# One kernel of four residual blocks on Trainium2: attention and retention of two mixers woven between weight units, gate sums and experts' one-hots moved

## The chip, the cores and the metric

The kernel runs on one core of one Trainium2 chip. Its five engines take instructions from queues of their own: TensorE (PE) multiplies, VectorE (DVE) and ScalarE (ACT) do elementwise work, GpSimd (POOL) and SyncE (SP) here only start DMAs. An engine runs its queue in the order in which the program was written; semaphores tie the queues together. The metric is the device time in microseconds of one execution; lower is better.

## The reference, cut to what matters

The input x is 256 rows by 1024. Everything is float32.

```
for l in 0, 1:                                  # first block
    mod = silu(c) @ ada_w[l] + ada_b[l]         # 6 vectors of 1024: sh1 sc1 g1 sh2 sc2 g2
    x += g1 * hybrid_mixer(rms_norm(x)*(1+sc1)+sh1)
    h  = rms_norm(x)*(1+sc2)+sh2
    x += g2 * (swiglu(h, 2816 wide) if l == 0 else moe_ffn(h))   # 8 experts, top 2
x = rms_norm(x)
for l in 0, 1:                                  # second block
    x += 0.5 * swiglu(rms_norm(x))              # ffn1, 2816 wide
    x += even_mixer(x) if l == 0 else odd_mixer(x)
    x += 0.5 * swiglu(rms_norm(x))              # ffn2
hybrid_mixer: h @ w_in (1024 x 3584) -> q k v of 8 heads of 64, q k v gate of 4 heads of 128
    causal softmax attention on the first, normed; rotary and decayed retention on the second,
    normed per head, times silu(gate); both side by side (1024) @ w_out (1024 x 1024)
```

## The kernel before

**Weights.** All weights pass through the core once, in *units* of 512 KB: 256 rows of a weight by 512 columns (or 128 rows by 1024). SP loads them into a ring of 12 raw buffers. A float32 product is made of three passes with rounded parts: ACT writes `hi`, the rounded weight (line 296), DVE writes `lo`, raw minus hi (line 298), and PE does hi by hi, hi by lo and lo by hi (`passes`, line 317, 128x512 each). There are SPL = 6 buffers of hi and of lo. So hi of unit u waits until PE has freed unit u-6; the semaphore `unit_free` counts that. How far ahead of PE the splits stand in the queues of ACT and DVE is written in the program: `split_to(n)` issues the splits up to unit n, `look_ahead(n)` the next n.

**Order of stages** (times of the profiled execution): conditioning to 60.8 us; hybrid mixer 0 to 240.9; dense ffn 0 to 476; hybrid mixer 1 483 to 655.9; routing to 705; the experts to 1530; then ffn1.0, the even mixer, ffn2.0, ffn1.1, the odd mixer and ffn2.1, which ends at 2622.

**Hybrid mixer.** `project` makes seven slabs of 512 columns with four units each; tile t = 0 of a slab (rows 0 to 127) is done for all four units, then t = 1. Heads are turned (transposed on PE) after the third and the sixth slab. Then `attention` runs 8 heads with no weights between them: scores on PE (line 1108), mask and maximum on DVE, two exps on ACT, a turn on PE (line 1154, 4 transposes), a copy on ACT, values on PE (line 1172). Two banks take turns for scores and two for turns. Retention follows, then the norms, and w_out (8 units) with `project_out`.

**Ada sums.** The vectors mod are products with one row, so DVE does them: it multiplies a 128x512 piece of `ada_w` by a column of c and adds it up (lines 270, 273, 844); PE then sums over partitions (lines 852, 957, 962). 32 units of `ada_w` lie in the raw ring between the weights of mixer 0 ("acc" units); the 12 slabs of layer 1 come by POOL's own DMAs, 11 of them beside the 11 steps of ffn 0 and the last beside mixer 1.

**Dense ffn.** A *step* takes six units: four for gate and up, 256 columns of the hidden each, and two for down of the step before. PE does gate and up of tile 0, the turn of the hidden (line 425), gate and up of tile 1, then down (`pe_down`), whose first product waits for `hidT_lo` (DVE, line 435), and that for `hidT_hi` (ACT, line 433). Each weight unit is freed in the part for tile 1, in down by its last product. After the last step `pe_down_last` does tile 0 and then tile 1, and the additions to x (DVE) and the next stage's first turns follow.

**Experts.** 88 steps of eight experts, 11 each, in the same manner for 128 rows. Two experts form a pair. At the second expert of a pair `one_hots(p+1)` (DVE, 4 instructions) and `gather` (PE, line 1746) prepare the next pair; at the first, `turn_one_hots` (PE, lines 1773 and 1776) prepares the way back.

## Time and profile before

| | us |
|---|---|
| median of 3 runs | 2629.36 (2629.26 to 2630.66) |
| the profiled execution, device time | 2626.93 |
| its span in the trace | 2625.7 |
| PE busy | 2383.0 (91%) |
| DVE busy | 1783.2 (68%) |
| ACT busy | 1377.8 (52%) |
| mean granted clock of TensorE | 0.924 of full |

Busy time is the union of an engine's instructions. A row that ends in brackets gives the idle time of the engine before it and the instruction that ended it. The three passes of a full-speed product start 0.2275 us apart, at half clock 0.427 us apart, though each is drawn 0.39 or 0.63 us long, since they overlap. A unit for both tiles is 12 passes, 2.73 us.

### The profile page before, as it was taken

The page shows a single profiled execution, that of the slowest core. Times are in us where ns is not written, and L with a number is a line of the kernel's source. Part 1 is how long each engine was busy: PE and PEld are TensorE (multiplying, and loading weights), DVE is VectorE, ACT ScalarE, POOL GpSimd, SP SyncE. Part 2 cuts the span into 40 slices and gives each one's busy share as a digit, 9 for nine tenths or more (in the row PEclk, how much of TensorE's full clock was granted, in tenths as well). Part 3 has the DMA queues.
Part 4 walks back from the last instruction along what each step waited for, and adds up shares of the span by engine and source line. Part 5 has one row for each costly group of instructions (what it writes and reads, how often), then busy time and mean ns, then how long its engine had stood idle before and what let it go on. Part 6 is the DMA issues. An engine that isn't in the chain of part 4 may idle for free.

```text
span 2625.7 us, 35352 instructions
## 1 busy us (share of the span) xinstructions
PE 2383.0 (91%) x10593; PEld 1953.9 (74%) x10593; DVE 1783.2 (68%) x2330; ACT 1377.8 (52%) x1955; POOL 47.9 (2%) x77
## 2 busy tenths in 40 slices
PE   6987899798499999999999979998899999869998
PEld 5766687677387877877878858876788788747887
DVE  5786777564398988988889965558555555575554
ACT  4333443243277767767767754444544544533543
POOL 1000111100000000000000000000000000000000
PEclk8968999897599999999999989998899999958999
DMA  8773788351199999999999955543356555311651
GB/s 293 238 240 100 263 299 301 107 176 40 49 346 315 368 308 328 356 311 363 318 308 368 368 188 191 188 154 127 122 184 190 164 188 179 131 56 44 196 182 59
DMA packets 410160, 571.51 MB, mean 218 GB/s; under 512 B 28103, under 2 KB 324465, under 8 KB 409938
## 3 DMA queue, kind: packets, MB, share of 16 engines
q1 hardware_dynamic: 399024, 538.94, 61.6%
q0 software_dynamic: 8112, 28.18, 3.6%
q10 hardware_dynamic: 2930, 3.22, 0.4%
q8 instruction: 50, 0.82, 0.1%
q14 instruction: 44, 0.36, 0.0%
HBM read 569.18 MB, written 1.05 MB: 217 GB/s over the span
## 4 chain that ended last, share of the span: by engine, by line
PE 80%; DVE 12%; ACT 4%; issue 2%; DMA 1%; SPq 0%; DVEq 0%; ACTq 0%; POOLq 0%
PE bank L317 70%; DVE lo L298 3%; PE bank L1108 1%; DVE small L90 1%; PE bank L1172 1%; DVE xn L90 1%; PE bank L425 1%; DVE proj L90 1%; PE bank L1746 1%; DVE aT_lo L90 1%; ACT xn L90 1%; PE bank L1154 1%; PE bank L1694 1%; DMA ada_slot<-ada_w 1%; DVE hT_full L90 1%
## 5 line engine op out<-in xcount | busy, mean ns | idle before, releaser
L298 DVE TENSOR_TENSOR lo<-raw,hi 128x1024 fp32r<-128x1024 f32 x997 | 1172.5, 1221 | 172.7 <-ACT hi L296 158.8
L296 ACT ACTIVATE hi<-raw 128x1024 fp32r<-128x1024 f32 x997 | 999.7, 1054 | 129.8 <-PE bank L317 121.7
L317 PE MATMUL bank<-hi,aT_hi 128*128 128x512 f32 (+2 forms) x2064 | 828.2, 401 | 20.0 <-DVE lo L298 9.2
L317 PE MATMUL bank<-hi,aT_lo 128*128 128x512 f32 (+2 forms) x2064 | 807.9, 391 | 0.0
L317 PE MATMUL bank<-lo,aT_hi 128*128 128x512 f32 (+2 forms) x2064 | 806.8, 391 | 0.0
L317 PEld LDWEIGHTS bank<-hi,aT_hi 128*128 128x128 f32 x2064 | 391.6, 190 | 104.6 <-issue 12.1
L317 PEld LDWEIGHTS bank<-hi,aT_lo 128*128 128x128 f32 x2064 | 390.5, 189 | 82.5
L317 PEld LDWEIGHTS bank<-lo,aT_hi 128*128 128x128 f32 x2064 | 391.9, 190 | 79.0 <-issue 3.1
L317 PE MATMUL bank<-hi,hidT_hi 128*128 128x512 f32 x792 | 315.6, 398 | 6.6 <-DVE hidT_lo L435 5.6
L317 PE MATMUL bank<-lo,hidT_hi 128*128 128x512 f32 x792 | 313.7, 396 | 0.0
L317 PE MATMUL bank<-hi,hidT_lo 128*128 128x512 f32 x792 | 312.9, 395 | 0.0
L317 PEld LDWEIGHTS bank<-hi,hidT_hi 128*128 128x128 f32 x792 | 152.6, 193 | 40.0 <-DVE hidT_lo L435 6.6
L317 PEld LDWEIGHTS bank<-hi,hidT_lo 128*128 128x128 f32 x792 | 152.0, 192 | 32.3
L317 PEld LDWEIGHTS bank<-lo,hidT_hi 128*128 128x128 f32 x792 | 152.0, 192 | 31.9 <-issue 0.5
L414 DVE SCALAR_TENSOR_TENSOR hid<-silu_g,r_keep,bank 128x256 f32<-128x256 f32 x88 | 41.9, 476 | 159.5 <-ACT silu_g L404 159.5
L404 ACT ACTIVATE silu_g<-bank,r_keep 128x256 f32<-128x256 f32 x88 | 41.5, 471 | 180.5 <-PE bank L317 180.5
L433 ACT ACTIVATE hidT_hi<-bank 128x512 fp32r<-128x512 f32 x55 | 32.9, 598 | 190.9 <-PE bank L425 190.9
L435 DVE TENSOR_TENSOR hidT_lo<-bank,hidT_hi 128x512 fp32r<-128x512 f32 x55 | 38.0, 691 | 129.6 <-ACT hidT_hi L433 129.6
L1682 ACT ACTIVATE silu_g<-bank 128x256 f32<-128x256 f32 x88 | 33.8, 384 | 116.1 <-PE bank L317 116.1
L844 DVE SCALAR_TENSOR_TENSOR ada_sum<-ada_slot,c_cols,ada_sum 128x512 f32<-128x512 f32 x84 | 63.1, 751 | 24.5 <-DMA ada_slot<-ada_w 22.3
L1686 DVE TENSOR_TENSOR hid<-silu_g,bank 128x256 f32<-128x256 f32 x88 | 36.8, 419 | 49.8 <-ACT silu_g L1682 46.4
L1108 PE MATMUL bank<-qkT 64*128 64x256 f32 (+1 forms) x160 | 61.2, 575 | 7.9 <-DVE small L90 3.9
(233 smaller groups left out, 1657.3 us busy)
## 6 DMA issues: line engine op xcount, KB each, us to landing
raw<-moe_w_gate SPq DMA_DIRECT2D x352, 256.0 KB
raw<-moe_w_up SPq DMA_DIRECT2D x352, 256.0 KB
raw<-moe_w_down SPq DMA_DIRECT2D x176, 512.0 KB
raw<-ffn_w_gu SPq DMA_DIRECT2D x352, 256.0 KB
raw<-ffn_w_down SPq DMA_DIRECT2D x110, 512.0 KB
raw<-w_in SPq DMA_DIRECT2D x56, 512.0 KB
raw<-ada_w SPq DMA_DIRECT2D x48, 512.0 KB
ada_slot<-ada_w POOLq DMA_DIRECT2D x48, 512.0 KB, 6.0
```

What stands on the lines that cost most here:

```text
L90: return self.did(op(*args, **kw))
L296: act.activation(hi[u % SPL][:, :], raw[r % RAW][:, :], ACTF.Copy).then_inc(hi_done, 1)
L298: dve.tensor_tensor(lo[u % SPL][:, :], raw[r % RAW][:, :], hi[u % SPL][:, :].bitcast(F32), ALU.subtract).then_inc(lo_done, 1)
L317: ins = pe.matmul(bank, left[a], right[b], start=first and n == 0, stop=last and n == 2)
L404: act.activation(silu_g[:, t, :], psum[t][:, 0:STEP_F], ACTF.Silu, scale=scale(t) if scale else 1.0).then_inc(ffn["ev"].silu, 1)
L414: ins = dve.scalar_tensor_tensor(out=hid[:, t, :], in0=silu_g[:, t, :], scalar=weight(t), in1=up, op0=ALU.mult, op1=ALU.mult)
L433: act.activation(hidT[0][:, :], psum[2][:, :], ACTF.Copy).then_inc(ffn["ev"].hi, 1)
L435: dve.tensor_tensor(hidT[1][:, :], psum[2][:, :], hidT[0][:, :].bitcast(F32), ALU.subtract).then_inc(ffn["ev"].lo, 1)
L844: ins = dve.scalar_tensor_tensor(out=acc[:, :], in0=src, scalar=c, in1=acc[:, :], op0=ALU.mult, op1=ALU.add)
L1108: ins = pe.matmul(psum[b][:, t * S:(t + 1) * S], q(h, mp, t), k(h, mp), start=True, stop=True)
L1682: act.activation(silu_g[:, g % 2, :], psum[g % 2][:, 0:STEP_F], ACTF.Silu).then_inc(ev.silu, 1)
L1686: dve.tensor_tensor(hid[:, g % 2, :], silu_g[:, g % 2, :], psum[g % 2][:, STEP_F:], ALU.mult)\
```

## The change

1. **Hybrid mixers.** After the first slab, each unit is used for both tiles at once (`slab_by_unit`), and behind each unit a function `slot(n)` puts a piece of other work, n being 4 times the slab plus the unit. Slots 8 and 9 turn q and k, slots 12 to 21 hold the eight heads (`causal_heads`: scores of head h, turn of h-1, values of h-2), slots 17 to 30 the rotary, retention and norms. The masked quarter of the scores is left out (3 transposes of 4), the mask is added by a product on PE, the scale is put on q. There is one bank for scores and one for turns. `w_out` comes in two halves: the attention's 512 rows in `out_first`, beside the retention's chain, the rest in `out_second`. All evacuations of slabs are ACT's. The six look-ahead splits stay filled after each unit (`split_ahead`).
2. **Ada sums.** 24 acc units lie in mixer 0 and 16 in mixer 1; ffn 0 has ten slabs. `last_slab` and `last_rows` are gone, and sums are closed as soon as they are complete.
3. **Dense ffn.** After the first gate and up, `split_to(u0 + UNITS_GU + SPL)` stands in place of `look_ahead(UNITS_GU)`: where two splits fewer were issued, all later ones of the ffn stand two units further ahead in the queues of ACT and DVE. `normed_*` issue the splits of four units after tile 0 of the turned input.
4. **Experts.** `one_hots(p+1)` moves ahead of the step at the boundary, `turn_one_hots` and `split_expert` from the second step to the third.

Cut to its core; `third_extra`'s call and the two unrolled steps are shown, new evacuations and tables are left out:

```diff
-ACC_SLABS = (4, 5, 6, 7, 8, 9, 10, 11)
...
+ACC_SLABS = [(0, n) for n in (4, 5, 6, 7, 8, 9)] + [(1, n) for n in (4, 5, 10, 11)]
+FFN_SLABS = [(0, 10), (0, 11)] + [(1, n) for n in (0, 1, 2, 3, 6, 7, 8, 9)]
...
+RAW_KINDS = ("s" * COND_UNITS + mix_kinds(lambda i: 2 if i == 35 else 1 if 8 <= i < 22 or 27 <= i < 35 else 0)
+             + "s" * FFN_UNITS + mix_kinds(lambda i: 1 if 8 <= i < 22 or 27 <= i < 29 else 0))
...
+    def split_ahead():
+        split_to(st["use"] + SPL)
...
+    def slab_by_unit(width, evacuate, banks, hook, left=aT, kd=KD, marks=()):
+        u = st["use"]
+        n_units = kd // 2
+        split_to(u + n_units)
+        PE.need(*marks, *(m for b in banks for m in bank_mark[b]))
+        for j in range(n_units):
+            pe.wait_ge(lo_done, split_end(u + j))
+            w = unit(u + j)
+            for t in range(NT):
+                for kk in range(2):
+                    k = 2 * j + kk
+                    ins = passes(psum[banks[t]][:, 0:width], [a[:, k, t * P:(t + 1) * P] for a in left],
+                                 [r[:, kk, 0:width] for r in w], k == 0, k == kd - 1)
+                if t == 0 and j == n_units - 1:
+                    mark0 = PE.did(ins)
+            ins.then_inc(unit_free, 1)
+            st["use"] += 1
+            if j == n_units - 1:
+                for t, mark in enumerate((mark0, (unit_free, u + n_units))):
+                    bank_mark[banks[t]] = evacuate(t, psum[banks[t]][:, 0:width], mark)
+            split_ahead()
+            hook(j)
...
+    def out_second(left, marks, gate, between):
+        u = st["use"]
+        split_to(u + 4)
+        PE.need(*marks)
+        for i in range(4):
+            pe.wait_ge(lo_done, split_end(u + i))
+            ins = out_unit(u, i, 0, left, False, True)
+        mark0 = PE.did(ins)
+        between()
+        for i in range(4):
+            out_unit(u, i, 1, left, False, True).then_inc(unit_free, 1)
+        st["use"] += 4
...
-        look_ahead(UNITS_GU)
+        split_to(u0 + UNITS_GU + SPL)
...
+        def scores(h):
+            e, nm = probs[:, h % 2, :], nmax[:, (h % 2) * NT:(h % 2 + 1) * NT]
+            PE.need(*bank_mark[4], *(marks() if h == 0 else ()))
+            pe.matmul(bank[:, 0:P], q(h, 0), k(h)[:, 0:P], start=True, stop=False)
+            pe.matmul(bank[:, 0:P], ident, mask, start=False, stop=True)
+            pe.matmul(bank[:, S:2 * S], q(h, 1), k(h), start=True, stop=False)
+            m = PE.did(pe.matmul(bank[:, S + P:2 * S], ident, mask, start=False, stop=True))
+            mx = [DVE.run([m, *ready.get(h - 2, ())], dve.tensor_reduce, nm[:, t:t + 1], bank[:, cut[t]], AX.X, ALU.max,
+                          negate=True) for t in range(NT)]
+            ready[h] = tuple(ACT.run([mx[1], *turned_of.get(h - 2, ())], act.activation, e[:, cut[t]], bank[:, cut[t]],
+                                     ACTF.Exp, bias=nm[:, t:t + 1], accum_out=rs[:, t * n + h:t * n + h + 1])
+                             for t in range(NT))
+            bank_mark[4] = (ready[h][1],)
+        def turn(h):
+            e = probs[:, h % 2, :]
+            PE.need(*ready[h], *bank_mark[5])
+            for i, at in enumerate((0, S, S + P)):
+                ins = pe.transpose(turn_bank[:, i * P:(i + 1) * P], e[:, at:at + P], ident)
+            turned_of[h] = (PE.did(ins),)
+            m = ACT.run([*turned_of[h], *pv_of.get(h - 2, ())], act.activation, probsT[:, h % 2, 0:3 * P],
+                        turn_bank[:, 0:3 * P], ACTF.Copy)
+            bank_mark[5] = (m,)
+        def values(h):
+            PE.need(*bank_mark[5], *(() if h else (*bank_mark[6], *bank_mark[7])))
...
+            pe.matmul(psum[6][:, at], pT[:, 0:P], v(h, 0), start=True, stop=True)
+            pe.matmul(psum[7][:, at], pT[:, P:2 * P], v(h, 0), start=True, stop=False)
+            pv_of[h] = (PE.did(pe.matmul(psum[7][:, at], pT[:, 2 * P:3 * P], v(h, 1), start=False, stop=True)),)
...
+        def part(i):
+            if i < n:
+                scores(i)
+            if 1 <= i <= n:
+                turn(i - 1)
+            if i >= 2:
+                values(i - 2)
...
+        def slot(n):
+            if n == 8:
+                turned_qk.extend(turn_pairs(lambda t, j: proj[:, t, j * P:(j + 1) * P], (4, 5), of(0), 0, 64 ** -0.5))
+            if n == 9:
+                turned_qk.extend(turn_pairs(lambda t, j: proj[:, t, SLAB + j * P:SLAB + (j + 1) * P], (6, 7), of(1), 4))
+            if 12 <= n < 22:
+                attend(n - 12)
+            if n in (17, 18):
+                rotate(3, n - 17)
+            if n in (20, 21):
+                rotate(4, n - 20)
+            if n == 22:
+                norm_attention()
+                chain["q"] = turn_pairs(lambda t, j: proj[:, t, 1536 + j * P:1536 + (j + 1) * P], (4, 5), rt[0:2], 8)
+            if n == 23:
+                chain["k"] = turn_pairs(lambda t, j: proj[:, t, 2048 + j * P:2048 + (j + 1) * P], (2, 3), rt[2:4], 12)
+            if n == 24:
+                PE.need(*chain["q"], *chain["k"])
+                ret_scores(0)
+                ret_scores(1)
+                oaT_marks.extend(turn_half(lambda t, k: xn[:, t, k * P:(k + 1) * P], (6, 7), o_a,
+                                           lambda k: col("att_out_g", 4 * layer + k), oaT))
+            if n == 25:
+                ret_values(0)
+                ret_values(1)
+                ret_scores(2)
+                ret_scores(3)
+            if n == 26:
+                ret_values(2)
+                ret_values(3)
+                ret_squares()
+            if n == 28:
+                ret_norm()
+            if n == 30:
+                chain["T"] = turn_half(lambda t, k: xn[:, t, SLAB + k * P:SLAB + (k + 1) * P], (0, 1), o_r,
+                                       lambda k: col("ret_out_g", 4 * layer + k), aT, 4)
+            close_accs(accs_ripe(), 5 if n < 28 else 1)
+        slab(SLAB, out_of_bank(0), turned)
...
+            if z == 1 and p < NE // 2 - 1:
+                one_hots(p + 1)
...
             def second_extra():
+                if z == 0 and p > 0:
+                    give_back(p - 1, 1)
+                if z == 1 and p < NE // 2 - 1:
+                    gather(p + 1, 1)
+            def third_extra():
                 if z == 0:
-                    split_expert(e + 1)
-                    if p > 0:
-                        give_back(p - 1, 1)
                     turn_one_hots(p)
-                elif p < NE // 2 - 1:
-                    gather(p + 1, 1)
+                if e < NE - 1:
                     split_expert(e + 1)
             step(g + 1, z, extra=first_extra, first=True)
             step(g + 2, z, extra=second_extra)
+            step(g + 3, z, extra=third_extra)
+            step(g + 4, z)
```

What stands in the queues now, at three places. First PE, in the attention of mixer 0. Before, the transposes of probs (L1154, the turn of head h-1) and the products of probsT and proj (values of head h-2) follow the scores (L1108, of head h):

```order
L1108 MATMUL bank<-qkT 128x256 [waits dve_count]
L1108 MATMUL bank<-qkT 128x256
L1154 MATMUL bank<-tables_sb,probs 128x128 [waits act_count]
L1154 MATMUL bank<-tables_sb,probs 128x128 x3
L1172 MATMUL bank<-proj,probsT 128x64 [waits act_count]
L1172 MATMUL bank<-proj,probsT 128x64 x2
L1108 MATMUL bank<-qkT 128x256 [waits dve_count]
L1108 MATMUL bank<-qkT 128x256
```

In the changed kernel one slot stands between the units. The first four rows are the scores with the mask, then three transposes, then the values; the last row is the next unit's first product:

```order
L1307 MATMUL bank<-qkT 128x128
L1308 MATMUL bank<-tables_sb 128x128
L1309 MATMUL bank<-qkT 128x256
L1310 MATMUL bank<-tables_sb 128x128
L1322 MATMUL bank<-tables_sb,probs 128x128 x3
L1331 MATMUL bank<-proj,probsT 128x64 [waits act_count]
L1332 MATMUL bank<-proj,probsT 128x64
L1333 MATMUL bank<-proj,probsT 128x64
L336 MATMUL bank<-hi,aT_hi 128x512 [waits lo_done]
```

What moved: the head stands between two units, and its values still wait for ACT (act_count). In the code that wait is `PE.need(*bank_mark[5])`, and bank 5's last mark is the copy of the turn just issued. On ACT, the same slot reads so (hi of a unit, the two exps of head h, the copy of the turn of head h-1):

```order
L313 ACTIVATE hi<-raw 128x1024 [waits unit_free,raw_full0]
L102 ACTIVATE probs,small<-bank,small 128x128 [waits dve_count]
L102 ACTIVATE probs,small<-bank,small 128x256
L102 ACTIVATE probsT<-bank 128x384 [waits pe_count]
```

Second ACT, in the loop of a dense ffn. Before (hidT_hi is what the next down needs):

```order
L404 ACTIVATE silu_g_54<-bank1,r_keep 128x256 [waits dense_hid]
L293 ISA
L295 REGISTER_ALU [waits raw_full2]
L296 ACTIVATE hi0<-raw2 128x1024 [waits unit_free]
L296 ACTIVATE hi1<-raw3 128x1024 [waits unit_free,raw_full3]
L431 ISA
L433 ACTIVATE hidT_hi_56<-bank2 128x512 [waits unit_free,dense_turned]
L399 REGISTER_ALU
L403 REGISTER_ALU [waits dense_gu]
L404 ACTIVATE silu_g_54<-bank0,r_keep 128x256 [waits dense_hid]
```

In the changed kernel, at the same place of the step:

```order
L502 ACTIVATE silu_g_54<-bank1,r_keep 128x256 [waits dense_hid]
L310 ISA
L312 REGISTER_ALU [waits raw_full0]
L313 ACTIVATE hi2<-raw0 128x1024 [waits unit_free]
L312 REGISTER_ALU [waits raw_full1]
L313 ACTIVATE hi3<-raw1 128x1024 [waits unit_free]
L529 ISA
L531 ACTIVATE hidT_hi_56<-bank2 128x512 [waits unit_free,dense_turned]
L497 REGISTER_ALU
L501 REGISTER_ALU [waits dense_gu]
L502 ACTIVATE silu_g_54<-bank0,r_keep 128x256 [waits dense_hid]
```

What moved: two hi of weights stand ahead of hidT_hi in both, but now they go to buffers 2 and 3 and not 0 and 1: they are the splits of two units later, and wait until PE has freed the units that held these buffers. DVE's lo stand in the same order.

Third DVE, at the boundary ahead of the second expert of a pair. Before:

```order
L1686 TENSOR_TENSOR hid<-silu_g,bank 128x256
L298 TENSOR_TENSOR lo<-raw,hi 128x1024 x2
L1702 TENSOR_TENSOR hidT_lo<-bank,hidT_hi 128x256
L298 TENSOR_TENSOR lo<-raw,hi 128x1024 x4
L90 TENSOR_SCALAR onehot<-tables_sb,slot_of 128x128 x4
```

In the changed kernel:

```order
L102 TENSOR_SCALAR onehot<-tables_sb,slot_of 128x128 x4
L1941 TENSOR_TENSOR hid<-silu_g,bank 128x256
L315 TENSOR_TENSOR lo<-raw,hi 128x1024 x2
L1957 TENSOR_TENSOR hidT_lo<-bank,hidT_hi 128x256
L315 TENSOR_TENSOR lo<-raw,hi 128x1024 x4
```

What moved: the four one-hots stand ahead of the hidden (hid) and of six lo, where before they stood behind the boundary's last lo.

## Rows read from the trace of the kernel before

**Rows 1.** page, parts 1 and 5
```profile
PE 2383.0 (91%) x10593; PEld 1953.9 (74%) x10593; DVE 1783.2 (68%) x2330; ACT 1377.8 (52%) x1955; POOL 47.9 (2%) x77
...
L298 DVE TENSOR_TENSOR lo<-raw,hi 128x1024 fp32r<-128x1024 f32 x997 | 1172.5, 1221 | 172.7 <-ACT hi L296 158.8
```

**Rows 2.** busy us (x) by stretch: PE, PEld, DVE, ACT, POOL; PEclk, DMA
```profile
152.00:198.00 46.00, 36.49 (x140) 29.36 (x139) 37.57 (x60) 14.81 (x42) 0.00 (x0) 0.56 0.70 227
198.00:218.90 20.90, 14.08 (x61) 10.40 (x60) 11.67 (x28) 6.28 (x15) 0.00 (x0) 0.66 0.15 49
218.90:240.90 22.00, 22.00 (x98) 17.92 (x96) 14.60 (x20) 10.72 (x14) 0.00 (x0) 1.00 0.36 115
...
577.10:611.20 34.10, 30.89 (x114) 24.39 (x113) 12.04 (x18) 14.63 (x42) 0.00 (x0) 0.55 0.17 53
611.20:633.00 21.80, 13.31 (x58) 12.01 (x58) 10.82 (x26) 6.63 (x15) 0.00 (x0) 0.66 0.00 0
...
713.00:1530.00 817.00, 788.31 (x3536) 649.31 (x3536) 706.60 (x750) 597.22 (x766) 0.00 (x0) 0.97 1.00 337
820.40:829.30 8.90, 4.01 (x19) 3.59 (x19) 5.26 (x8) 2.20 (x3) 0.00 (x0) 0.65 1.08 366
```

**Rows 3.** PE in time, attention: start us, us, operation, [idle <-releaser]
```profile
156.29 0.63 PE L1154 MATMUL bank<-tables_sb,probs 128*128 128x128 f32 x4 [2.71 <-ACT probs L90]
...
160.71 1.09 PE L1154 MATMUL bank<-tables_sb,probs 128*128 128x128 f32 x4 [2.37 <-ACT probs L90]
...
584.86 1.38 PE L1172 MATMUL bank<-proj,probsT 128*128 128x64 f32 x6
...
589.08 1.17 PE L1172 MATMUL bank<-proj,probsT 128*128 128x64 f32 x5
```

**Rows 4.** DVE in time, attention of mixer 1
```profile
578.98 0.69 DVE L90 TENSOR_REDUCE small<-probs 128x2 f32<-128x512 f32 x1
```

**Rows 5.** ACT in time, attention of mixer 1
```profile
577.81 1.28 ACT L90 ACT_TABLE_LOAD   x1
579.70 0.51 ACT L90 ACTIVATE probs<-probs,small 128x256 f32<-128x256 f32 x1 [0.60 <-DVE small L90]
...
582.06 0.60 ACT L90 ACTIVATE probsT<-bank 128x512 f32<-128x512 f32 x1
```

**Rows 6.** ACT in time, one step of ffn1 of layer 0
```profile
1642.15 0.60 ACT L433 ACTIVATE hidT_hi<-bank 128x512 fp32r<-128x512 f32 x1 [3.43 <-PE bank L425]
...
1643.55 1.06 ACT L296 ACTIVATE hi<-raw 128x1024 fp32r<-128x1024 f32 x1 [0.43 <-PE bank L317]
1644.90 1.06 ACT L296 ACTIVATE hi<-raw 128x1024 fp32r<-128x1024 f32 x1 [0.30 <-PE bank L317]
```

**Rows 7.** DVE in time, the same step
```profile
1642.78 0.69 DVE L435 TENSOR_TENSOR hidT_lo<-bank,hidT_hi 128x512 fp32r<-128x512 f32 x1 [2.61 <-ACT hidT_hi L433]
...
1644.64 5.31 DVE L298 TENSOR_TENSOR lo<-raw,hi 128x1024 fp32r<-128x1024 f32 x4 [0.78 <-ACT hi L296]
```

**Rows 8.** the chain that ended last, ffn 0, then plain ffn: start, us
```profile
317.18 0.86 PE bank L852 x2
...
1642.11 16.36 PE bank L317 x72
```

**Rows 9.** PE in time, ends of a plain ffn and of ffn 0
```profile
455.13 0.66 PE L425 MATMUL bank<-tables_sb,hid 128*128 128x128 f32 x4 [2.62 <-DVE hid L412]
...
1647.43 0.39 PE L317 MATMUL bank<-hi,hidT_hi 128*128 128x512 f32 x1
...
1747.40 1.03 PE L682 MATMUL bank<-tables_sb,x_res 128*128 128x128 f32 x8
```

**Rows 10.** DVE in time, end of the plain ffn
```profile
1744.85 1.42 DVE L90 SCALAR_TENSOR_TENSOR x_res<-bank,x_res 128x512 f32<-128x512 f32 x2 [2.08 <-PE bank L317]
```

**Rows 11.** PE in time, two boundaries between experts
```profile
825.71 0.58 PE L1746 MATMUL bank<-onehot,xn_hi 128*128 128x256 f32 x1 [4.89 <-DVE onehot L90]
...
940.24 0.69 PE L1773 MATMUL bank<-tables_sb,onehot 128*128 128x128 f32 x2 [3.85 <-DVE ysum L90]
```

More of the change, by code:

```diff
@@ new lines, in out_loads, with out_unit @@
+    def out_loads(w):
+        for part in range(2):
+            for half in range(2):
+                for k in (4 * part, 4 * part + 2):
+                    v = w[k * P:(k + 2) * P, half * SLAB:(half + 1) * SLAB].rearrange("(k p) n -> p k n", p=P)
+                    load((lambda r: r[:, :].rearrange("p (k n) -> p k n", k=2), v))
+    def out_unit(u, i, t, left, first, last):
+        half, kp = i // 2, i % 2
+        w = unit(u + i)
+        for kk in range(2):
+            k = 2 * kp + kk
+            ins = passes(psum[4 + 2 * t + half][:, :], [a[:, k, t * P:(t + 1) * P] for a in left],
+                         [r[:, kk, :] for r in w], first and k == 0, last and k == 3)
+        return ins
@@ L747, in second @@
             return tile(1)
-        return {"marks": [tile(0), None], "second": second}
+        ACT.did(act.activation(tiny(1), eps_col[:, :], ACTF.Sqrt))
+        first = tile(0)
+        split_to(st["use"] + 4)
+        return {"marks": [first, None], "second": second}
     def normed_plain(gain):
@@ L985, in last_rows @@
[L985 to L993 removed]
+            gates_mark[:] = [DVE.run([(ada_rows, 2), gates_in[0]], dve.tensor_tensor, gates[:, 1, :], gates[:, 1, :], mod_rows[:, 0:D], ALU.add)]
@@ new lines, in turn_pairs @@
+    def turn_pairs(src, banks, marks, at, scale=None):
+        PE.need(*marks)
+        done = []
+        for j in range(0, 4, 2):
+            b = banks[j // 2]
+            PE.need(*bank_mark[b])
+            for jj in range(2):
+                for t in range(NT):
+                    ins = pe.transpose(psum[b][:, jj * S + t * P:jj * S + (t + 1) * P], src(t, j + jj), ident)
+            m = PE.did(ins)
+            dst = qkT[:, at + j:at + j + 2, :].rearrange("p j s -> p (j s)")
+            if scale:
+                m = ACT.run([m, *marks], act.activation, dst, psum[b][:, :], ACTF.Copy, scale=scale)
+            else:
+                m = DVE.run([m, *marks], dve.tensor_copy, dst, psum[b][:, :])
+            bank_mark[b] = (m,)
+            done.append(m)
+        return done
@@ L1253, in hybrid_mixer @@
[L1253 to L1265 removed]
+        for c in range(7):
+            proj_load(io["w_in"][layer], c * SLAB, SLAB)
@@ new lines, in hybrid_mixer, with out_of_bank, evacuate, of @@
+        out_loads(io["w_out"][layer])
+        m, rt, turned_qk, o_a, oaT_marks, decayed, pv, o_r, chain = {}, [], [], [], [], {}, {}, [], {}
+        def out_of_bank(c):
+            def evacuate(t, bank, mark):
+                m[c, t] = ACT.run([mark], act.activation, proj[:, t, c * SLAB:(c + 1) * SLAB], bank,
+                                  ACTF.Silu if c == 6 else ACTF.Copy)
+                return (m[c, t],)
+            return evacuate
+        def of(*cs):
+            return [m[c, t] for c in cs for t in range(NT)]
@@ L1291, in hybrid_mixer @@
[L1291 to L1296 removed]
+            pe.matmul(psum[2][:, h * P:(h + 1) * P], sT[:, 0:P], vr[0], start=True, stop=True)
@@ new lines, in ret_values, with ret_squares @@
+            pe.matmul(psum[3][:, h * P:(h + 1) * P], sT[:, P:S], vr[0], start=True, stop=False)
+            pv[h] = (PE.did(pe.matmul(psum[3][:, h * P:(h + 1) * P], sT[:, S:S + P], vr[1], start=False, stop=True)),)
+        def ret_squares():
+            ss = tiny(NT * 4)
+            a = [ACT.run([*pv[3], *o_a, *oaT_marks], act.activation, xn[:, t, SLAB:], psum[2 + t][:, :], ACTF.Square)
+                 for t in range(NT)]
+            chain["ss"] = ss
+            chain["sums"] = [DVE.run([a[t]], dve.reduce_sum, ss[:, t * 4:(t + 1) * 4],
+                                     xn[:, t, SLAB:].rearrange("p (n d) -> p n d", n=4), axis=AX.X) for t in range(NT)]
```

269 lines of the change are left out of this document (155 added, 114 removed).

## The prediction

> **What bounds the kernel.** I read the page first: PE is busy 91% of the span, no other engine over 68% [rows 1]. The time is PE's work plus the stretches where PE stands or runs at half clock, so I looked for these. The busy times by stretch [rows 2] show them: in the two attentions the granted clock is 0.56 and 0.55 (its levels are 1.2 and 2.4 GHz, so nearly all of it at 1.2), in the two retentions PE is busy 14 of 21 us. w_out (22.0 us for 96 passes) and the experts (788 of 817 us busy) are nearly pure work. PE in order of time [rows 3] shows the attention: a wait of 2.71 us at its start, one of 2.37 behind it, and from there one head per 4.22 us (584.86 to 589.08) with no gap, at half clock. Between experts PE waits 4.89 us for the one-hots and 3.85 us for ysum [rows 11]. Everything is set against the profiled execution, 2626.93 us (span 2625.7); the median of the runs shown is 2.4 above it. Unless said otherwise a sum is of full clock.
>
> **Mixers.** Weight units cost 2.73 us. Thirteen of 28 are done before slot 12; the 15 behind them and 1.75 us of turns end at 152.4 and 577.1, so slot 12 stands at about 109.7 and 534.4. In mixer 1 the last slab's products (0.86 us a slab in ffn 0 [rows 8]), its additions and the wait on them go; I take 2.7 for them, so 531.7. From there 131.2 and 121.5 us were left to the ends at 240.9 and 655.9.
>
> One head's PE work is 2.1 us (half of 4.22); two mask products more, one transpose and a quarter of the scores less, I take 2.35. A slot with its unit would be 5.1. But values of head h-2 wait for the copy of head h-1, which ACT does behind the exps of head h, these behind DVE's maxima, and these behind the unit's lo. From the unit's last pass: 0.3 to hi, 1.06 for hi [rows 6], 1.22 for lo [rows 1], so 2.65; two maxima of 128 and 256 columns, less than the 0.69 of 512 columns [rows 4], 0.6; two exps of 0.51 and less with their accumulators, 1.0, and the copy 0.5 (0.60 for 512 columns [rows 5]). That is 4.75, while PE has 1.2 of scores and 0.45 of turns. It stands 3.0 us, and the slot is 8.1. Before, the wait was for an older copy in the other bank, and ACT had no hi in between. Six slots have all three parts (48.6), the four at the edges take 16. Then ten slots to the second half of w_out: 27.3 of units, 7 of PE's turns, scores and values, and 9.8 of stalls, since sums of ada, rotary, norms and the 1.28 us table load [rows 5] stand in one chain across ACT and DVE: 44 in mixer 0, 40 in mixer 1, where few sums are left at that place. The second half of w_out is 11.6. So 120 and 116: ends at 229.9 and 648, 11 and 8 earlier.
>
> The clock is the second term. It fell behind waits of 2.71 and 2.37 us [rows 3]; the slots now have waits of 3.0 us every 8. At half clock throughout a slot takes 11.4 (twice 5.1, less a stall that shrinks to about 1), 20 us more over six; at full clock nothing. I take 10 each, 12 in all, and 3 for the ten slots behind. Mixer 0 comes to +4, mixer 1 to +7. Bounds: if nothing is lost to the clock -11 and -8, if all is +13 each.
>
> The Trainium skill has a rule for this term: its page "ScalarE: Activation LUTs", section "What ACT_TABLE_LOAD costs", puts a switch at 1.28 us plus a drain of 1.38. Here the load is 1.28 and starts 0.02 behind the activation before it, so no drain is seen; by the page mixer 0, with one load more than before, would be 3 us worse and not 1.
>
> **Dense ffn, the steps.** A plain step has 72 passes of 16.36 [rows 8] and a turn of 0.44: 16.80. hidT_hi began at 1642.15 [rows 6], far ahead of the need at 1647.43 [rows 9]. Now the two hi ahead of it wait for units freed in gate and up of tile 1: these are the rows at 1643.55 and 1644.90. So hidT_hi starts at 1645.96 or a little before. DVE's lo of that second unit starts at 1645.99 and stands ahead of hidT_lo: 1647.13, and with 0.69 [rows 7] and its signal PE goes at 1647.87. That is 0.44 late, and with 0.11 for the restart (no row shows it better than 0.0 to 0.2) 0.55 a step: ten steps in each of four plain ffns, +22. It is hidden where DVE's lo run 0.4 us quicker, so 0 is the lower end, 28 the upper.
>
> **Dense ffn, the ends.** Before, the last hi of a ffn stood ahead of the additions without a wait. Two units deeper, the last two hi wait for the end of `pe_down_last`, since it frees both units only with tile 1. PE went on at once at 1747.40 with turns of x [rows 9], for which the additions of tile 0 had run at 1744.85 in 1.42 [rows 10]. Now DVE has the two lo ahead of them: 1747.4 + 0.3 + 2x1.06, then the last lo, 1750.0, additions to 1751.4. That is +4.05, and 1.7 for the clock behind such a wait, in three ends (into the even mixer, into ffn1.1, into the odd mixer): +17. Bounds 0 and 20. At ffn 0's end the same is given back, since the late additions have no lo ahead any more: 0.
>
> **ffn 0.** It has the 0.55 too, and its sums (0.86 on PE a step [rows 8]) stand behind a deeper lo, so 1.2 a step, +12, and +2 at its start; its last step no longer waits 2.62 for the last slab [rows 9] nor has its 2.07 product: -5. Sum +9, bounds 0 and 16. Eight of the 48 pieces that went by POOL's queue and eight of mixer 0's 32 now go by the raw ring in mixer 1, 8 MB; there the DMA share was 0.17 in the attention [rows 2], which covers them; uncovered they would cost 8 MB, some 25 us, which I hold unlikely.
>
> **Experts.** The one-hots stand six lo and a boundary ahead, so the wait of 4.89 goes, and with it the half clock behind it: 820.4 to 829.3 [rows 2] has 16 products of 0.21 that take 0.11 at full clock and some of the next, 2.1. In the third step turn_one_hots no longer waits 3.85 for ysum, and 2.5 of half clock. 13.4 for each of three pairs: -39. DVE has 706.6 us of work in 817, so it has time for what it did in these waits; if a quarter of it comes back as a wait for lo, -28. The upper end is -43.
>
> **Sum.** +4 +7 +22 +17 +9 -39 = +20; 2647, on the medians 2649.
>
> **Rivals.**
> - *The other side, faster than before: the deeper look-ahead costs nothing.* Its place is the step of the dense ffn, its price the terms +22, +17 and 12 of ffn 0, and it decides from the point where the lo ahead of hidT_lo ends before 1646.7. If DVE's lo start early enough, steps, ends and the 12 in ffn 0 go: 51 less, so 2649-51 = 2598. For it: PE waits nowhere in a plain step now. Against it: the chain is of durations of single rows and its first link is PE's own unit. 0.17.
> - *The regimes fill each other.* With no stalls a mixer is 41 and 33 us shorter, as PE then has only work at full clock; experts and ffns as above: 20-11-74 = -65, so 2564. The woven slots have PE work of 5.1 and a chain of 4.75, which could run beside the next unit if values waited for an older copy. Against it: the order of the three rows on PE. 0.08. Of it the Trainium skill says ("Perfetto Trace Analysis", section "Optimization Strategy") that "performance may be improved by interleaving those regimes"; its rule is for regimes that another engine bounds, and here in attention PE at half clock was the bound, not ACT or DVE, busy 12 and 15 of 34 us.
> - *Slower still: the clock stays down through slots 12 to 31 and behind the experts' boundaries.* Mixers +13 and +13 in place of +4 and +7, and of the experts' 13.4 a pair only 6 is gained, -18 in place of -39: +15+21, 2685. For it: the clock stayed down through the whole attention once it had fallen, though PE was without a gap there. Against it: the slots have fewer small products in a row. 0.15.
> - *The change doesn't do what it says in the experts*: the wait moves to the gather's reader: -39 turns into -10, 2678; within the case above and the range.
>
> **How the numbers follow.** The forecast, all terms within their own bounds near the values taken, 0.50; the first rival 0.17, the second 0.08, the third 0.15, and 0.10 for mixtures with smaller ffn costs around 2625. The time is 2649. Around it the case's own range is 2632 to 2667. The 8 in 10 go from 2592 to 2684, which leaves out the second rival and the upper edge. What a measurement of this kernel can tell from no change is about 0.2%, 5.3 us: faster is below 2624.1 (0.17 + 0.08 + some of the mixtures, 0.28), same 0.11, slower 0.61.
>
> **What would show it.** Right: in the profile after, a slot of 8 to 11 us from product to product of weights in slots 14 to 19, PE idle 2 to 3 us before values with ACT's copy as its releaser; a wait of 0.4 to 0.5 us for hidT_lo in each plain step and a period of 17.3 us; 4 us in front of the turns at the three ends; no wait at the odd boundary of experts. Wrong: a plain step of 16.80, which takes 39 to 51 us off the sum; or slots of 5 to 6 us at full clock.

## The result and the profile after

The changed kernel takes 2681.03 us (median of 4 runs, 2674.95 to 2685.43), the kernel before 2630.01 (4 runs): a ratio of 1.0192, 95% interval 1.0172 to 1.0213. It is slower by 51 us; forecast was 2649, slower by 20. The direction and most of the mechanisms held, the size did not: the time lies inside the range (2592 to 2684), but near its upper edge, and the change is 2.6 times the one forecast.

The page's first part, the first line of part 5, the span and two stretches of the changed kernel (answering to [rows 1] and [rows 2]; the first stretch holds the slots with heads in mixer 0, the second the experts):

```profile
span 2678.9 us, 34900 instructions
...
PE 2398.5 (90%) x10641; PEld 1940.6 (72%) x10641; DVE 1757.6 (66%) x2347; ACT 1369.3 (51%) x1966; POOL 42.5 (2%) x69
...
L315 DVE TENSOR_TENSOR lo<-raw,hi 128x1024 fp32r<-128x1024 f32 x997 | 1177.8, 1221 | 618.2 <-ACT hi L313 613.9
```

```profile
118.00:172.00 54.00, 42.99 (x171) 31.22 (x169) 17.07 (x35) 15.70 (x38) 0.00 (x0) 0.81 0.29 89
757.00:1530.00 773.00, 770.61 (x3528) 635.33 (x3529) 703.76 (x749) 596.38 (x766) 0.00 (x0) 1.00 1.05 355
```

The experts' stretch is full now: PE busy 770.6 of 773 us, clock 1.00, where it was 788 of 817 at 0.97. DVE's idle time ahead of lo has risen from 172.7 [rows 1] to 618.2 us: it waits for hi, and hi for units that PE has yet to free. That points to splits that stand further ahead in the queue; what it costs, the line does not say (it is 247.3 us in experiment 1, but 526.4 in experiment 4, where no step waits).

To see which stage lost, compare the same event in both kernels: PE's first turn of x behind a stage (line 682 before, 781 after). Before, then after:

```profile
242.40 0.77 PE L682 MATMUL bank<-tables_sb,xn 128*128 128x128 f32 x5 [1.47 <-DVE xn L90]
...
480.77 0.44 PE L682 MATMUL bank<-tables_sb,xn 128*128 128x128 f32 x2 [4.35 <-DVE xn L90]
...
657.39 0.88 PE L682 MATMUL bank<-tables_sb,xn 128*128 128x128 f32 x6 [1.47 <-DVE xn L90]
```

```profile
250.20 0.98 PE L781 MATMUL bank<-tables_sb,xn 128*128 128x128 f32 x7
...
511.86 0.47 PE L781 MATMUL bank<-tables_sb,xn 128*128 128x128 f32 x1 [7.61 <-DVE xn L102]
...
696.63 0.55 PE L781 MATMUL bank<-tables_sb,xn 128*128 128x128 f32 x3 [1.11 <-DVE xn L102]
```

The experts end where PE first waits for the last hidden (it goes on at 1524.40 before, at 1527.61 after). With the spans this makes:

| stretch | before | after | difference | forecast |
|---|---|---|---|---|
| to the end of mixer 0 | 242.4 | 250.2 | +7.8 | +4 |
| ffn 0 | 238.4 | 261.7 | +23.3 | +9 |
| mixer 1 | 176.6 | 184.8 | +8.2 | +7 |
| routing and experts | 867.0 | 831.0 | -36.0 | -39 |
| second block | 1101.3 | 1151.3 | +50.0 | +39 |
| sum | | | +53.2 | +20 |

**A woven slot.** PE, then ACT, then DVE of the changed kernel, slots 14 and 15 of mixer 0:

```profile
121.11 0.49 PE L1322 MATMUL bank<-tables_sb,probs 128*128 128x128 f32 x3
123.72 0.43 PE L1331 MATMUL bank<-proj,probsT 128*128 128x64 f32 x2 [2.12 <-ACT probsT L102]
...
133.75 0.43 PE L1331 MATMUL bank<-proj,probsT 128*128 128x64 f32 x2 [2.54 <-ACT probsT L102]
```

```profile
119.49 1.06 ACT L313 ACTIVATE hi<-raw 128x1024 fp32r<-128x1024 f32 x1 [0.76 <-PE bank L336]
122.37 0.37 ACT L102 ACTIVATE probs<-bank,small 128x128 f32<-128x128 f32 x1 [1.82 <-DVE small L102]
...
123.18 0.49 ACT L102 ACTIVATE probsT<-bank 128x384 f32<-128x384 f32 x1
```

```profile
120.58 1.23 DVE L315 TENSOR_TENSOR lo<-raw,hi 128x1024 fp32r<-128x1024 f32 x1 [1.74 <-ACT hi L313]
121.72 0.61 DVE L102 TENSOR_REDUCE small<-bank 128x1 f32<-128x128 f32 x2
```

This is the forecast chain link by link: hi, lo, maxima, exps, copy, values, 4.5 us behind the unit. The wait is 2.1 to 2.5 us instead of 3.0, because the scores with their masks take 1.8 us and not 1.2, and the chain is 0.2 shorter. From 123.72 to 133.75 it is 10.0 us a slot; the prediction's sum has 9.8 (8.1 and a sixth of the 10 taken for the clock). The granted clock was at its lower level for 3.4 us behind five of the six waits, and 0.81 on the mean of the stretch.

**A plain step of a dense ffn**, ACT, DVE and PE (answering to [rows 6, 7, 9]):

```profile
1630.39 1.06 ACT L313 ACTIVATE hi<-raw 128x1024 fp32r<-128x1024 f32 x1 [5.85 <-PE bank L336]
1631.75 1.06 ACT L313 ACTIVATE hi<-raw 128x1024 fp32r<-128x1024 f32 x1 [0.30 <-PE bank L336]
1632.72 0.58 ACT L531 ACTIVATE hidT_hi<-bank 128x512 fp32r<-128x512 f32 x1
```

```profile
1631.48 2.59 DVE L315 TENSOR_TENSOR lo<-raw,hi 128x1024 fp32r<-128x1024 f32 x2 [5.66 <-ACT hi L313]
1633.99 0.68 DVE L533 TENSOR_TENSOR hidT_lo<-bank,hidT_hi 128x512 fp32r<-128x512 f32 x1
```

```profile
1634.80 0.49 PE L336 MATMUL bank<-hi,hidT_hi 128*128 128x512 f32 x1 [0.37 <-DVE hidT_lo L533]
```

The chain that ended last of two steps earlier (start, us, what; answering to [rows 8]):

```profile
1582.44 11.16 PE bank L336 x48
1593.60 0.44 PE bank L523 x4
1594.04 2.76 PE bank L336 x12
...
1596.83 1.07 ACT hi L313
...
1599.06 0.69 DVE hidT_lo L533
...
1599.88 11.16 PE bank L336 x48
```

hidT_hi, which before started 5 us ahead of the need, now follows two hi that wait for PE, and PE waits 0.37 us for hidT_lo. The chain leaves PE between its 12th and its last passes of gate and up and comes back for down: 3.08 us by ACT and DVE where PE needs 2.73 for its work. The 48 passes behind the wait take 11.16 us, where 48 at 0.2275 take 10.92, so the restart is 0.24 and more, and the period is 17.44 to 17.47 for 16.80.

**The end of ffn1.0**, DVE and PE (answering to [rows 9] and [rows 10]):

```profile
1757.12 2.58 DVE L315 TENSOR_TENSOR lo<-raw,hi 128x1024 fp32r<-128x1024 f32 x2 [6.97 <-ACT hi L313]
1759.62 1.41 DVE L102 SCALAR_TENSOR_TENSOR x_res<-bank,x_res 128x512 f32<-128x512 f32 x2
```

```profile
1748.14 0.66 PE L523 MATMUL bank<-tables_sb,hid 128*128 128x128 f32 x4 [2.80 <-DVE hid L512]
...
1761.09 1.97 PE L781 MATMUL bank<-tables_sb,x_res 128*128 128x128 f32 x8 [3.79 <-DVE x_res L102]
```

The second row of PE is the forecast wait for the additions. The first was not forecast: the last turn of the hidden waits 2.80 us, 1.08 before, since a hi that waits stands ahead of the silu too.

### The profile page after: what moved, and what is told of

Read it like the earlier page. It is cut to its first block, busy times and chain, and to the rows that moved or that the text cites. A ratio compares the mean times of both kernels' runs of the same rounds, so it can differ in the third digit from the quotient of the medians.

```text
span 2678.9 us, 34900 instructions
## 1 busy us (share of the span) xinstructions
PE 2398.5 (90%) x10641; PEld 1940.6 (72%) x10641; DVE 1757.6 (66%) x2347; ACT 1369.3 (51%) x1966; POOL 42.5 (2%) x69
## 4 chain that ended last, share of the span: by engine, by line
PE 73%; DVE 13%; ACT 7%; issue 5%; DMA 2%; DVEq 0%; SPq 0%; ACTq 0%
PE bank L336 63%; ACT hi L313 3%; DVE lo L315 3%; DVE hidT_lo L533 1%; DVE small L102 1%; DVE xn L102 1%; PE bank L523 1%; DVE acc_sum L950 1%; DVE proj L102 1%; DMA ada_slot<-ada_w 1%; ACT xn L102 1%; PE bank L1949 1%; PE bank L1268 1%; PE bank L2001 1%; DVE x_res L102 1%
## 5 line engine op out<-in xcount | busy, mean ns | idle before, releaser
L315 DVE TENSOR_TENSOR lo<-raw,hi 128x1024 fp32r<-128x1024 f32 x997 | 1177.8, 1221 | 618.2 <-ACT hi L313 613.9
L336 PE MATMUL bank<-hi,aT_hi 128*128 128x512 f32 x2032 | 830.3, 409 | 18.9 <-DVE aT_lo L102 8.9
L336 PE MATMUL bank<-hi,aT_lo 128*128 128x512 f32 x2032 | 804.2, 396 | 0.0
L336 PE MATMUL bank<-lo,aT_hi 128*128 128x512 f32 x2032 | 803.3, 395 | 0.0
L1955 ACT ACTIVATE hidT_hi<-bank 128x256 fp32r<-128x256 f32 x88 | 33.9, 386 | 50.3 <-PE bank L1949 50.3
L102 ACT ACTIVATE probs<-bank,small 128x128 f32<-128x128 f32 (+1 forms) x64 | 28.0, 443 | 61.5 <-DVE small L102 61.4
L523 PE MATMUL bank<-tables_sb,hid 128*128 128x128 f32 x220 | 34.2, 278 | 26.9 <-DVE hid L510 17.4
L950 DVE SCALAR_TENSOR_TENSOR acc_sum<-ada_slot,c_cols,acc_sum 128x512 f32<-128x512 f32 x70 | 52.6, 751 | 8.5 <-DMA ada_slot<-ada_w 5.8
L523 PEld LDWEIGHTS bank<-tables_sb,hid 128*128 128x128 f32 x220 | 26.3, 141 | 38.5 <-DVE hid L510 22.1
L292 DVE SCALAR_TENSOR_TENSOR acc_sum<-raw,c_cols,acc_sum 128x512 f32<-128x512 f32 x70 | 52.4, 749 | 1.5
L512 DVE SCALAR_TENSOR_TENSOR hid<-silu_g,r_keep,bank 128x256 f32<-128x256 f32 x88 | 41.7, 473 | 13.4 <-ACT silu_g L502 13.4
```

Source lines behind the costliest of these rows:

```text
L102: return self.did(op(*args, **kw))
L292: ins = dve.scalar_tensor_tensor(out=acc[:, :], in0=src, scalar=c, in1=acc[:, :], op0=ALU.mult, op1=ALU.add)
L315: dve.tensor_tensor(lo[u % SPL][:, :], raw[r % RAW][:, :], hi[u % SPL][:, :].bitcast(F32), ALU.subtract).then_inc(lo_done, 1)
L336: ins = pe.matmul(bank, left[a], right[b], start=first and n == 0, stop=last and n == 2)
L512: ins = dve.scalar_tensor_tensor(out=hid[:, t, :], in0=silu_g[:, t, :], scalar=weight(t), in1=up, op0=ALU.mult, op1=ALU.mult)
L523: ins = pe.transpose(psum[2][:, f * S + t * P:f * S + (t + 1) * P], hid[:, t, f * P:(f + 1) * P], ident)
```

## The experiments

Each kernel was timed beside the kernel before; a median is of 4 executions where no other number is given. Three undo or repair one part, one joins them, one changes a size, two do a part of the experts' change alone, one tries more, two show what the weave alone is worth.

**1. The look-ahead as before.**

```diff
-        split_to(u0 + UNITS_GU + SPL)
+        split_to(u0 + UNITS_GU + 4)
```

> The changed kernel with the look-ahead of the dense ffns two units shallower, as before. My theory (the deeper splits gate PE): the period of a plain step goes from 17.47 back to 16.80 and its wait of 0.37 us for hidT_lo is gone, 10 x 0.67 in each of four ffns, 27 us; the three plain ends lose their 3.79 us wait for the additions and some of the 2.80 for hid, 7 us each, 21; in ffn 0 the steps lose 12 and the start 2.6. Together 2681 - 62 = about 2619. Rival (the extra time is the two mixers' and the clock's, and the small waits of a step would show up elsewhere): under 20 us gained, 2661 or more.

Measured 2607.9 us (2601.0 to 2612.6), ratio to before 0.992 (0.9903 to 0.9937). That is 73 us under the changed kernel, for 62 expected and over three times the rival's 20. A plain step reads, from the chain that ended last (start, us, what):

```profile
1611.67 0.44 PE bank L523 x4
1612.10 16.36 PE bank L336 x72
```

and the turns of x at ffn1.0's end follow with no wait:

```profile
1717.39 1.03 PE L781 MATMUL bank<-tables_sb,x_res 128*128 128x128 f32 x8
```

From PE's wait ahead of the second tile of ffn1.0 to the end the spans are 1071.1 before, 1122.4 after and 1075.0 here: 47 us are the four plain ffns and their ends. ffn 0 gives 26: from turn to turn 235.7 us, 2.6 less than before, for 261.7. These two make the 73; the two profiled executions are 79 apart, and the other 6 lie in stretches that the edit leaves as they are (4.0 of them ahead of ffn 0). So this one line cost more than the whole change lost.

**2. Values wait for their own copy.**

```diff
-            bank_mark[5] = (m,)
+            bank_mark[5] = copied[h] = (m,)
...
-            PE.need(*bank_mark[5], *(() if h else (*bank_mark[6], *bank_mark[7])))
+            PE.need(*copied[h], *(() if h else (*bank_mark[6], *bank_mark[7])))
```

> The changed kernel with one mark changed: the values of head h-2 wait for the copy of their own head and not for the copy of the head after it. My theory (the wait in bank 5's mark is what stalls a woven slot): the waits of 2.1 to 2.5 us ahead of the values go, in slots 14 to 19 of both mixers, and with them the 3.4 us at half clock that follow each; a slot falls from 10.0 to 5.6 us, 6 x 4.4 x 2 = 53 us: about 2628. If a stall only moves to the scores (one bank) or to lo, the slot stays at 8 or more: 2657 or more. Rival on the clock alone (it falls whatever the waits are): slot 10.0 to 7.5, 2651.

Measured 2631.8 us (10 runs, 2628.9 to 2636.0), ratio 1.0004 (0.9994 to 1.0013): 49 us under the changed kernel, 53 expected. PE in the same slots, and the same stretch:

```profile
121.30 0.49 PE L1322 MATMUL bank<-tables_sb,probs 128*128 128x128 f32 x3
121.63 0.33 PE L1331 MATMUL bank<-proj,probsT 128*128 128x64 f32 x2
...
127.28 0.33 PE L1331 MATMUL bank<-proj,probsT 128*128 128x64 f32 x2
...
132.93 0.33 PE L1331 MATMUL bank<-proj,probsT 128*128 128x64 f32 x2
...
135.30 0.85 PE L1069 MATMUL bank<-ones_sq,acc_sum 128*128 128x1 f32 x4 [1.59 <-ACT probsT L102]
```

```profile
118.00:172.00 54.00, 50.51 (x249) 39.19 (x247) 29.14 (x57) 21.55 (x51) 0.00 (x0) 0.94 0.42 126
```

A slot is 5.65 us, and the stretch holds 249 products instead of 171 at a clock of 0.94 for 0.81. The wait was there only by its mark, and the clock followed the waits. One wait is left, 1.59 us ahead of a product that closes a sum of ada. Its row names ACT's copy of the turn, and not DVE's sum: the closing goes to bank 5, whose mark is that copy, so this is again a wait on a shared bank.

**3. The splits of normed_* behind the late additions.**

```diff
         def second():
             run_late()
+            split_to(st["use"] + 4)
...
-        split_to(st["use"] + 4)
```

> The changed kernel with the splits of normed_* issued behind the late additions instead of ahead of them. My theory for what I had not foreseen (the 8.95 us at ffn 0's start against 4.75 before, and 13.75 against 9.54 at the routing): two lo, 2.4 us, stand ahead of the additions of tile 1 at the ends of the two hybrid mixers; the gap falls by about 2 to 4 us at each, and the ends of the plain ffns, where these splits are already issued, don't change. 2681 - 6 = 2675. Rival: the gap is the longer chain of the second tile itself and stays: 2681; or the lo now stand in the chain of tile 1: no gain.

Measured 2675.4 us (2671.7 to 2677.8), ratio 1.0174 (1.0157 to 1.0191), 5.7 us under the changed kernel. By the medians alone this is not far outside the spread of either; the traces decide it. PE behind the late additions (those to tile 1 of x) in ffn 0 and DVE around them, first of the changed kernel, then here, then DVE in the kernel before:

```profile
265.05 1.33 PE L781 MATMUL bank<-tables_sb,xn 128*128 128x128 f32 x5 [8.95 <-DVE xn L102]
```

```profile
257.49 2.36 DVE L315 TENSOR_TENSOR lo<-raw,hi 128x1024 fp32r<-128x1024 f32 x2 [0.52 <-ACT hi L313]
259.76 0.68 DVE L102 TENSOR_TENSOR xn<-bank,gates 128x512 f32<-128x512 f32 x1
...
261.81 0.69 DVE L102 TENSOR_TENSOR x_res<-x_res,xn 128x512 f32<-128x512 f32 x1
```

```profile
258.06 1.97 PE L781 MATMUL bank<-tables_sb,xn 128*128 128x128 f32 x8 [6.74 <-DVE xn L102]
```

```profile
252.13 0.68 DVE L102 TENSOR_TENSOR xn<-bank,gates 128x512 f32<-128x512 f32 x1
...
254.79 2.35 DVE L315 TENSOR_TENSOR lo<-raw,hi 128x1024 fp32r<-128x1024 f32 x2
257.06 0.16 DVE L102 RECIPROCAL small<-small 128x1 f32<-128x1 f32 x1
```

```profile
249.08 0.68 DVE L90 TENSOR_TENSOR xn<-bank,gates 128x512 f32<-128x512 f32 x1
249.79 0.69 DVE L90 TENSOR_TENSOR x_res<-x_res,xn 128x512 f32<-128x512 f32 x1
```

The wait falls from 8.95 to 6.74, and at the routing from 13.75 to 11.51. The same places had 4.75 and 9.54 before: about half of a cost of 4.2 us at each of two places is got back. The rows tell what the other half is. Before, one pair of additions stood at this place (1.4 us); in the changed kernel there are two, 259.76 to 262.50, 1.4 us more, which no place of the splits can give back. The splits cost the other 2.8: 2.36 of lo and the wait for their hi. Moved behind the additions they still cost 0.6, since the reciprocal of the second tile stands behind the two lo (it comes 2.2 us after the last addition, 1.55 before).

**4. One unit deeper in place of two.**

```diff
-        split_to(u0 + UNITS_GU + SPL)
+        split_to(u0 + UNITS_GU + 5)
```

> The changed kernel with the dense ffns' look-ahead one unit deeper than before, in place of two. My theory, by the chain that gates a step: only one hi, which waits for the first unit freed in gate and up of tile 1, stands ahead of hidT_hi, and its lo ends 1.3 us before the down needs hidT_lo; so the plain step is back at 16.80 and the 27 us of the steps are gone, as with none deeper. At a ffn's end one hi waits for the first unit freed by pe_down_last, 1.37 us before its end, and one lo: additions about 0.5 to 1 us late, so 1 to 2 us of each end's 7 remain. In sum 5 us above the 2607.9 of none deeper: 2613. Rival (each unit of depth costs half, through the load on ACT and DVE): steps of 17.1 and half of 73: 2644.

Measured 2624.2 us (10 runs, 2616.2 to 2633.7), ratio 0.9977 (0.9964 to 0.999). The steps are as the chain says, the sum is 11 us worse than expected. Here are the chain in a plain step and PE at the end of ffn1.0:

```profile
1608.89 0.44 PE bank L523 x4
1609.32 16.38 PE bank L336 x72
```

```profile
1733.99 1.09 PE L781 MATMUL bank<-tables_sb,x_res 128*128 128x128 f32 x8 [2.44 <-DVE x_res L102]
```

With one waiting hi ahead of hidT_hi there is no wait in a step: it is a threshold of the queue, not a load on ACT and DVE, which was the rival. The ends were mis-sized: a wait of 2.44 us, for the 0.5 to 1 expected, with the lower clock in 1725.2 to 1728.6, as in the first experiment, and again in 1735.4 to 1738.8. Against the first experiment the three ends cost 3.8, 3.6 and 4.9, 12 in all, and ffn 0 takes 7.3 more (at its start PE waits 9.44 us against 8.11, at its end 6.26 against 2.59).

**5. The three edits together.** The edits of 1, 2 and 3.

> The changed kernel with the three edits together: look-ahead of the dense ffns as before, values waiting for their own copy, splits of normed_* behind the late additions. My theory: three separate prices, so they add: 73 + 49 + 6 = 128 off 2681, 2553. Rival (they share the clock, so that part of each gain was the same time): 2565 or more.

Measured 2554.1 us (2550.4 to 2556.5), ratio to before 0.9714 (0.9698 to 0.973), 1 us from the sum of the three. It is the fastest kernel of this study, 76 us under before and 127 under the changed one. PE is busy 2345.7 us, 92% of 2549.1.

**6. The experts' part alone, on the kernel before.** The edit is part 4 of the change.

> The kernel before with the experts' part of the change alone: one_hots ahead of the boundary, turn_one_hots and split_expert in the third step. My theory: the part is worth all that the experts' stretch gained in the changed kernel, 42 us: 2588. Rival (part of it comes from what stands before it in the ring or from the time at which the experts start): 20 to 30 us, 2600 to 2610.

Measured 2587.0 us (2584.2 to 2593.1), ratio 0.9838 (0.9821 to 0.9854): -43.5. None of the six waits at the experts' boundaries is left.

**7. Only the one-hots of it.**

```diff
             z, p, g = e % 2, e // 2, STEPS * e
+            if z == 1 and p < NE // 2 - 1:
+                one_hots(p + 1)
...
                 if z == 1 and p < NE // 2 - 1:
-                    one_hots(p + 1)
                     gather(p + 1, 0)
```

> The kernel before with only one_hots(p+1) moved ahead of the boundary step, the rest of the experts' part as before. My theory: the wait of 4.89 us for the one-hots and the half clock behind it go at three boundaries, 7 each: 2630 - 21 = 2609, and the waits of 3.85 for ysum stay. Rival (the four one-hots or their lo reappear as a wait of the hidden): 2615 or more.

Measured 2609.2 us (2607.8 to 2613.5), ratio 0.9919 (0.9902 to 0.9935): -21.0. The three waits of 3.84 us for ysum are still there, at 935, 1136 and 1338, each with 6.8 us at the lower clock behind it; the ones for the one-hots are gone. So the move of the one-hots is worth 21.0 and the rest of the part 22.5.

**8. Sums closed one unit later.**

```diff
-        return max(0, (st["acc"] - 2) // 4)
+        return max(0, (st["acc"] - 3) // 4)
```

> The three edits together, and the sums of ada closed one acc unit later. In the kernel with its own copies one woven slot still waits 1.6 us for the DVE sum that PE closes, and half clock follows for 6.8 us. My theory: that wait goes, 1.6 + 3, in mixer 0, less in mixer 1: 4 to 6 us under the three edits alone, 2548. Rival: the closing meets another late sum: the same as without it.

A miss: 2563.0 us (2562.2 to 2563.6), ratio 0.9745 (0.9729 to 0.9761), 9 slower than experiment 5. The wait of 1.6 us in the slot did go. But the closing of another slab moved into slot 22, behind the norm of the attention and the turns. PE and DVE there, then PE in experiment 5:

```profile
171.82 1.84 PE L1069 MATMUL bank<-ones_sq,acc_sum 128*128 128x1 f32 x8 [9.14 <-DVE qkT L102]
```

```profile
170.39 1.28 DVE L102 COPY qkT<-bank 128x512 f32<-128x512 f32 x2
```

```profile
174.77 1.94 PE L1367 MATMUL bank<-tables_sb,proj 128*128 128x128 f32 x8 [4.59 <-ACT proj L102]
```

DVE had done its part of the sum by 164.5. What the closing waits for is bank 5 once more: slot 22 turns q into banks 4 and 5, and DVE empties them with its copies to qkT, behind the whole norm of the attention. Since PE's queue is in order, the next unit's 12 passes wait behind the closing. The same wait of 9.14 us stands in mixer 1, so the mixers take 7.2 and 6.6 us more than in experiment 5. The expectation took the wait of 1.6 us for one on DVE's sum; by the rows it was on the bank.

**9. The weave alone.** Experts as before, look-ahead as before: what is left are the woven mixers, the moved sums and the splits of normed_*.

> The changed kernel without its experts' part and without the deeper look-ahead: what is left is the weave of the two mixers, the moved sums of ada and the splits of normed_*. My theory (the prices add): 2607.9 and the experts' 43.5 back, 2651, 21 above the kernel before: woven as written, the mixers cost time. Rival (the weave pays, and only the look-ahead hid it): 2630 or less.

Measured 2650.6 us (2640.4 to 2654.7), ratio 1.007 (1.0043 to 1.0097): 20 slower than before.

**10. The weave with its two repairs.** Experiment 9 with the edits of 2 and 3.

> The same, and the values wait for their own copy and the splits of normed_* stand behind the late additions. My theory: 2554.1 + 43.5 = 2598, so the weave is worth 32 us once it has no false wait. Rival (the weave's gain in the three edits' kernel is partly the experts'): 2610 or more.

Measured 2600.2 us (2595.3 to 2602.6), ratio 0.988 (0.9864 to 0.9897): 31 faster than before. So the same weave costs 20 us or gives 31, by one mark and the place of the splits at two stage ends, and the prices add within 3 us.

## Why the prediction was off

The forecast was +20 and +51 was measured. Of the 31 us between them the deeper look-ahead makes 21, the ends of the two hybrid mixers 8, and the mixers themselves 5 the same way; the experts gave 4 more than forecast.

**The deeper look-ahead: right mechanism, mis-sized.** This is the main term of the sum that failed. The prediction gave it +22 for the steps, +17 for the ends and, in ffn 0, 12 and part of 2, about 52; the first experiment measured 73.

- *Steps, +27 for +22.* A step costs 0.67 and not 0.55: the wait is 0.37 for 0.44, but the restart behind it is 0.24 to 0.3 and not 0.11.
- *Ends, +23 for +17.* From one turn of x for tile 1 to the next the three ffns take 208.9, 207.6 and 207.3 us for 195.2, 193.4 and 191.9; less 6.7 for the steps, the ends cost 7.1, 7.4 and 8.7 and not 5.75. The silu ahead of the last turn also stands behind a hi that waits, 2.80 for 1.08: I had followed only the queue behind the last product and not the one ahead of it. The clock adds its part: the changed kernel has 10.2 us at the lower level at each of these ends, the kernel before 3.4 at the first two and none at the third, the dearest. The wait for the additions came out near the forecast (3.79 for 4.05) by two errors that cancel: the sum holds both hi until the last product of `pe_down_last`, though the first needs only the unit freed 1.36 us earlier (1756.03 and 1757.39 on ACT), and it gives the last lo 0.2 us, where one takes 1.2.
- *ffn 0, +26 for 12 and part of 2.* Against experiment 1 its start (from the turn of x to the first turn of the hidden) is 3.0 longer, the steps up to the last turn of the hidden 14.7 and the end 8.2. "The same is given back" was wrong: there too a hi that waits for `pe_down_last` stands ahead of the late additions (PE waits 7.61 us, 2.59 in experiment 1). The 5 us that the prediction took off for the last slab are real, but only experiment 1 shows them: there the end takes 21.1 us for 25.6 before, in the changed kernel 29.3.

**The ends of the two hybrid mixers: a term put at nothing.** I named the splits of normed_* in the change and gave them no price, and did not see the second pair of late additions. Together they cost 4.2 us at the end of either mixer, 2.8 and 1.4. That is where the routing's gain of 39 came out at 36: the experts' stretch itself gained more (from PE's last wait of the routing to the end of the experts 814.2 before, 773.5 after, -40.7, and 1.5 behind it).

**The mixers: right.** +4 and +7 were forecast, +7.8 and +8.2 measured. Mixer 0 is known only to some 4 us: it ends between 245.5 and 250.2 in the changed kernel and in experiments 1, 3, 4 and 9, which don't edit it. The slot of 10.0 us and its cause are as worked out, though two errors cancel in it: scores of 1.8 for 1.2 us, and a wait of 2.1 to 2.5 for 3.0. The reading of the attention before was of two mixers taken as one: the wait of 2.37 is mixer 0's, which has two more over 1 us (2.06 and 1.51), and the row of heads without a gap is mixer 1's. Three slips of its sums move nothing: 121.5 us belongs to 534.4 and not to 531.7 (124.2), a slot at half clock is 11.2 by its own terms and not 11.4, and 4.75 less 1.65 is 3.1 and not 3.0.

**The experts: right**, -39 for -43.5 alone (three pairs of 13.4 are 40). DVE had the time, and the half clock behind the waits went with them.

**The rivals.** The first (the look-ahead costs nothing) is excluded by experiment 1. The second (the regimes fill each other) is excluded for the kernel as written, by the 10.0 us of a slot, and partly right for the kernel with its own copies: experiment 10 shows 31 us of gain, not the 74 that the rival had. One mark stood in the way of that much; no run shows what holds back the rest. By experiments 9 and 10 the Trainium skill's advice to interleave regimes ("Perfetto Trace Analysis", section "Optimization Strategy") pays here only once the marks between the queues allow it. Against this rival the prediction said that ACT and DVE were busy 12 and 15 of 34 us: it is DVE 12 and ACT 15, and in mixer 0 DVE was as busy as PE (37.6 and 36.5 of 46 us [rows 2]). The third (the clock stays down, experts gain half) gave nearly the right time, 2685, for wrong reasons: in the woven slots the clock is back 3.4 us later, and the experts gained everything. A time near a rival's is no sign that its mechanism is at work.

One stretch tells how far two single traces can be read. From the first turn of the normed input to the turns of x the odd mixer takes 142.7 us before and 145.5 after, and between 142.4 and 146.8 in the ten experiments, none of which edits this stretch. A difference of 3 us in one stretch of two traces is not yet a finding.

## What to carry to other kernels

Count for each split that is issued early what it waits for, and then read what stands behind it in both queues. One more unit of look-ahead was free in the steps and cost about 4 us at each end; two cost 0.67 us in each of 40 steps and 7 to 9 us at each end. A mark that belongs to a bank names its last user, not the data: when work is woven more tightly, let each reader wait for its own producer. And put no product into a bank that another engine is about to empty at the end of its longest chain: all that stands behind it in PE's queue waits too.
